# Both halves of the token operand, interleaved by k at fixed places modulo 256 bytes

## What is computed

```python
h = rmsnorm(x, g_pre)                        # x: 288 tokens x 2048
proj = einsum('btd,dn->btn', h, w_in)        # w_in: 2048 x (10 * 2048 + 16)
q, k, v, o, za, ig, fg, u, vb, zb, ga, gb = split(proj)
...                                          # mLSTM on q,k,v (8 heads of 256); spatial gating on u,vb
y_a = sigmoid(o) * hn * silu(za)
y_b = spatial_gating(u, layernorm(vb)) * silu(zb)
merged = sigmoid(ga) * (y_a @ w_pa) + sigmoid(gb) * (y_b @ w_pb)
y = x + rmsnorm(merged @ w_out, g_post)
```

## Time and profile before

| | |
|---|---|
| median of 3 runs | 1470.55 us (1470.46 to 1470.95) |
| the profiled execution's own time | 1470.46 us |
| span of the profile | 1469.0 us |
| TensorE busy with matmuls | 1453.8 us, 99% of the span |
| VectorE, ScalarE, GpSimd busy | 863.1, 622.6, 189.5 us |
| granted TensorE clock, mean | 0.997 |

### The profile page before, as it was taken

The page is one execution under the profiler, slowest core; times in us unless marked ns, Lnnn a source line. Parts: engine busy times, 40 slices in busy tenths (PEclk is TensorE's granted clock), DMA queues, the critical chain, the costliest instruction groups (busy, mean ns, idle before and its releaser), DMA issues. The chain is left out here.

```text
span 1469.0 us, 31016 instructions
## 1 busy us (share of the span) xinstructions
PE 1453.8 (99%) x11115; PEld 1432.7 (98%) x11115; DVE 863.1 (59%) x1418; ACT 622.6 (42%) x869; POOL 189.5 (13%) x340
## 2 busy tenths in 40 slices
PE   9999999999999999999999999999999999999996
PEld 9999999999999999999999999999999999999996
DVE  7756555564444437586767676767676544444444
ACT  6433343343333334454544444445454433333442
POOL 4000000001000000404040414141412000000000
PEclk9999999999999999999999999999999999999998
DMA  7764655557555568696969696969696665655553
GB/s 230 227 155 138 180 161 166 162 151 248 179 174 171 183 184 212 168 293 175 303 166 301 173 305 171 302 174 300 173 289 165 216 174 178 176 177 191 170 156 138
DMA packets 310679, 292.14 MB, mean 199 GB/s; under 512 B 82881, under 2 KB 297609, under 8 KB 309841
## 3 DMA queue, kind: packets, MB, share of 16 engines
q1 hardware_dynamic: 291424, 243.05, 59.1%
q0 software_dynamic: 18960, 48.48, 9.7%
q10 hardware_dynamic: 256, 0.10, 0.0%
HBM read 266.11 MB, written 25.44 MB: 198 GB/s over the span
## 5 line engine op out<-in xcount | busy, mean ns | idle before, releaser
L1066 DVE TENSOR_TENSOR wlo<-raw,whi 128x1024 fp32r<-128x1024 f32 x416 | 506.8, 1222 | 525.3 <-ACT whi L802 523.7
L453 PE MATMUL ps<-xh,whi 128*128 128x288 f32 x2560 | 762.8, 298 | 0.0
L454 PE MATMUL ps<-xl,whi 128*128 128x288 f32 x2560 | 757.4, 296 | 0.0
L455 PE MATMUL ps<-xh,wlo 128*128 128x288 f32 x2560 | 753.8, 294 | 0.0
L802 ACT ACTIVATE whi<-raw 128x1024 fp32r<-128x1024 f32 x416 | 439.3, 1058 | 690.4 <-PE ps L455 656.1
L453 PEld LDWEIGHTS ps<-xh,whi 128*128 128x128 f32 x2560 | 481.4, 188 | 4.9 <-issue 2.9
L454 PEld LDWEIGHTS ps<-xl,whi 128*128 128x128 f32 x2560 | 481.2, 188 | 0.4
L455 PEld LDWEIGHTS ps<-xh,wlo 128*128 128x128 f32 x2560 | 481.1, 188 | 0.0
L453 PE MATMUL ps<-yh,whi 128*128 128x288 f32 x512 | 151.4, 296 | 0.0
L454 PE MATMUL ps<-yl,whi 128*128 128x288 f32 x512 | 151.4, 296 | 0.0
L455 PE MATMUL ps<-yh,wlo 128*128 128x288 f32 x512 | 150.4, 294 | 0.0
(11 more groups left out here) (345 smaller groups left out, 1020.7 us busy)
## 6 DMA issues: line engine op xcount, KB each, us to landing
raw<-in_w_in_dram SPq DMA_DIRECT2D x320, 512.0 KB, 3.9
raw<-in_w_pb_dram SPq DMA_DIRECT2D x32, 512.0 KB, 3.5
Cin<-in_state_mlstm_C_dram POOLq DMA_DIRECT2D x16, 1024.0 KB, 8.4
Xb<-in_state_mlstm_C_dram SPq DMA_DIRECT2D x256, 64.0 KB, 3.8
out_dram<-Cin POOLq DMA_DIRECT2D x16, 1024.0 KB, 6.4
raw<-in_w_pa_dram SPq DMA_DIRECT2D x32, 512.0 KB, 3.5
raw<-in_w_out_dram SPq DMA_DIRECT2D x32, 512.0 KB, 3.6
bcs<-rows_d POOLq DMA_DIRECT2D x8, 304.0 KB, 3.7
```

Of the source, the lines that this page charges most:

```text
L453: nc.tensor.matmul(out, whi[:, c, kk, cols], mh_[:, k, :], start=(k == 0), stop=False)
L454: nc.tensor.matmul(out, whi[:, c, kk, cols], ml_[:, k, :], start=False, stop=False)
L455: last = nc.tensor.matmul(out, wlo[:, c, kk, cols], mh_[:, k, :], start=False, stop=(k == KT - 1))
L1066: nc.vector.tensor_tensor(wlo[:, c], raw[:, c], whi[:, c].bitcast(F32), ALU.subtract).then_inc(lo_ready, 1)
```

## The change

The two halves of each token operand become one tensor with k outside and the half inside: `xx[P, KT, 2, T]`, of which `xh` and `xl` are views, and so `yy` and `mm`. Row k of the upper half now starts at base + 2,304 k and that of the lower half 1,152 bytes after it. 2,304 is 9 times 256, and `moving` now gives an address that is 64 modulo 256, so the upper rows are at phase 64 for every k and the lower rows at phase 192. The weights' area is rounded to 256 instead of 128; it was at 0 modulo 256 before and stays there, one step of 256 further up, and all behind it moves by 256 bytes too. No instruction is added or taken away; addresses and, for writes of two k at once, the distance between the two rows change (2,304 bytes in place of 1,152).

```diff
     def moving(at):
-        return (at + 63) // 128 * 128 + 64
+        return (at + 191) // 256 * 256 + 64
 
     fixed = Area(moving(base))
-    xh = fixed("xh", [P, KT, T], F32R)
-    xl = fixed("xl", [P, KT, T], F32R)
-    fixed = Area((fixed.at + 127) // 128 * 128)
+    xx = fixed("xx", [P, KT, 2, T], F32R)
+    xh, xl = xx[:, :, 0, :], xx[:, :, 1, :]
+    fixed = Area((fixed.at + 255) // 256 * 256)
...
-    yh = y_("yh", [P, KT, T], F32R)
-    yl = y_("yl", [P, KT, T], F32R)
+    yy = y_("yy", [P, KT, 2, T], F32R)
+    yh, yl = yy[:, :, 0, :], yy[:, :, 1, :]
...
-    mh = a("mh", [P, KT, T], F32R)
-    ml = a("ml", [P, KT, T], F32R)
+    mm = a("mm", [P, KT, 2, T], F32R)
+    mh, ml = mm[:, :, 0, :], mm[:, :, 1, :]
```

## The result

The changed kernel takes 1479.05 us, median of 6 runs (1478.67 to 1479.86), against 1470.55 us before: ratio 1.0056, 95% interval 1.0046 to 1.0066. It is slower by 8.5 us: the interval lies above 1.

What follows compares the result with a forecast made beforehand. The prediction took TensorE's matmul pitch as the bound: 1470.5 us less 14.0 us for the moving operand's new phases, all else counted as nothing, gave 1456.5 us. The range was 1432 to 1480 us, the likeliest case's own 1446 to 1467.

Steps and rivals of the forecast that it cites:

- the 0.2% that I had called no change: Whole kernel time: 0.2%, 2.9 us, was about what a measurement can tell from no change.
- The bound: TensorE: nothing keeps it waiting, so the time is the number of matmuls, 9,984, times their pitch, mean 132.5 ns.
- Supply, writes and DMA: Weight supply has over half its time to spare; ScalarE and VectorE writes of two k and DMA transfers: nothing counted.
- gate_sums: Its 32 matmuls would change under 0.1 us; its 131.9 ns pitch was read as one unit saved per phase change pair.
- The unit: Matmul pitch moves in steps of 16 columns, 64 bytes, 16 cycles, 6.67 ns, below 133.33 ns.
- part (1): Moving operand, all 9,984 matmuls: a phase change pair every three matmuls saves one 6.67 ns step, 131.1 ns, -14.0 us.
- (a): Rival on matmul pitch: phase changes save two 6.67 ns steps per pair, 128.9 ns, 1434.5 us; chance 0.18.
- Part (4): Weight loads: weights keep their phase; the new order of moving phases against them was left in the uncertainty, no size.
- Rival (b): Matmul pitch: the phase itself counts, 64 cheap and 192 dear (1469.5 us), or phases do not count (1470.5); chance 0.17.
- Rival (c): Matmul pitch: a change saves only what a run of one phase built up, so 133.33 ns, 1478.8 us; chance 0.20.
- (d): Matmul pitch: a single matmul at 192 between two at 64 costs one step more, 135.6 ns, 1501 us; chance 0.08.

Runs made afterwards that it cites:

- b_h64l192: Layout and order of the kernel before, upper rows read from those at 64, lower rows from those at 192 (wrong rows): 1479.03 us, before 1470.62.

## Why two thirds at the good place save nothing

In the changed kernel two of three matmuls stand at relative 64, and all pay 133.33. Three runs on that:

> Changed kernel; the lower row's matmul comes first of the three (lower with whi, upper with whi, upper with wlo). The sequence of phases is the same but for where it begins (192 64 64); what differs is which weights are loaded beside it. If the sequence of phases alone decides: 133.33 ns, 1479 us. If it matters that the lower row stands between two upper ones with the same weights before it: another pitch, down to 132.2 ns, 1468 us.

> Changed kernel; in one k first the four matmuls with the upper row, then the two with the lower row: runs of four at 64 and two at 192, still two thirds at 64. If what the good phase saves is lost because runs are too short: less than 133.33 ns, 132.2 at best, 1468 us. If runs of even length lose it (runs of two did): 133.33 ns, 1479 us.

> Layout and order of before, upper rows read from those at 192, lower rows from those at 64 (wrong rows, weights at 0). Against the weights this is the sequence that the changed kernel had with its weights at 128. If the relative place and its sequence decide: that kernel's 132.5 to 132.6 ns and 1472 us. If only the share of matmuls at relative 64 counts (a third): 132.9 ns or more, 1475 us.

```diff
-    [(kk, j, w) for kk in range(CK) for j in range(2) for w in (0, 1, 2)]
+    [(kk, j, w) for kk in range(CK) for j in range(2) for w in (1, 0, 2)]
...
+    [(kk, j, w) for kk in range(CK) for j, w in ((0, 0), (0, 2), (1, 0), (1, 2), (0, 1), (1, 1))]
```

(The first new order is a_lfirst, the second a_run4, both in the changed kernel; b_h192l64 is the layout of before with PHASES = (192, 64).) 1478.33, 1477.78 and 1471.67 us, beside 1470.85. In that order:

```profile
380.00:523.00 143.00, 143.00 (x1074) 143.00 (x1074) 57.55 (x50) 51.01 (x51) 2.71 (x5) 1.00 0.57 175
```

```profile
380.00:523.00 143.00, 143.00 (x1074) 143.00 (x1074) 57.42 (x51) 50.89 (x51) 2.71 (x5) 1.00 0.57 175
```

```profile
380.00:523.00 143.00, 143.00 (x1080) 143.00 (x1080) 58.51 (x50) 50.74 (x52) 2.72 (x5) 1.00 0.58 175
```

133.4, 133.4 and 132.7 ns. So it isn't which weights are loaded beside the lower row, nor that the lower row stands alone. That runs of even length lose the saving, the other branch for a_run4, fits runs of two and four but not those of six and twelve. And b_h192l64, with one third at the good place, saves where two thirds don't; it agrees with the changed kernel with moved weights (1472.34 us, the same count of 1,080), which has the same relative sequence 192 64 192. The price of a matmul isn't a sum over places: the sequence has its own.

## Three kernels with all their work

None of these leaves out or changes any product. The first keeps every row at relative place 64 against its own slice, by giving the weight slices of odd k another phase than those of even k:

```diff
...
-    whi = fixed("whi", [P, CHUNKS, CK, PW], F32R)
+    fixed = Area(fixed.at + 128)
+    whi = fixed("whi", [P, 2, 8 * PW + 32], F32R)      # even k, then odd k 128 bytes further on; wlo too
...
-        return (at + 63) // 128 * 128 + 64
+        return (at + 63) // 256 * 256 + 192
```

> Correct kernel. Token operands in the layout of before, but yh and mh moved so that all of them begin at 192 modulo 256; whi and wlo keep the slices of even k from 128 modulo 256 and those of odd k from 0. So every token row starts 64 past the place of its weight slice modulo 256, whatever k. If the relative place sets the pitch: 131.7 ns as in the run with weights at 128 and rows at 192, and the time that it had, 1463 us, a ratio of 0.995. If it only held because all rows and all slices stood still: 132.5 ns or more, 1470 us.

1472.83 us against 1470.85, ratio 1.0011, interval 1.0002 to 1.0020. Its stretch:

```profile
380.00:523.00 143.00, 143.00 (x1079) 143.00 (x1078) 58.48 (x50) 50.52 (x52) 2.71 (x5) 1.00 0.57 175
```

132.8 ns, one unit in twelve. The expected 131.7 didn't come. While the last matmul of a k runs, the slice being loaded is the next k's, 128 bytes off in phase; one load in six is at relative 192. That this breaks the pattern is argued from the schedule and not shown by a run of its own.

The second has the token operands at 0 modulo 128, weights at 0 (the diff of the section on the weights' place), and the order of before, so relative places 128 and 0 alternate by k:

> Correct kernel: layout and order of before with the token operands at 0 modulo 128, so that rows start in turn at 128 and at 0 modulo 256, six matmuls each. If only relative place 192 is dear: 131.7 to 132.2 ns, 1463 to 1468 us, faster than before. If 128 is dear as well: like before, 132.2 to 132.8 ns, 1468 to 1473 us, or 133.33 ns and 1479 us if the changes of place cost what the good phase saves.

1473.56 us against 1470.68, ratio 1.0019, interval 1.0010 to 1.0028. Its stretch:

```profile
380.00:523.00 143.00, 143.00 (x1079) 143.00 (x1078) 58.47 (x50) 50.53 (x52) 2.72 (x5) 1.00 0.56 175
```

132.8 ns. A six at 0 and a six at 128 save one unit between them, no more than 64 and 192 in their slow pattern.

The third is the order with runs of three, timed:

> Correct kernel: layout of before, TensorE's order with runs of three (one k and one j, then k+1), timed. The single look gave 1468.1 us with 132.2 ns a matmul in nearly every chunk. Both theories expect the ratio to the kernel before at 0.998 and to hold in every run, since no disturbance enters it.

1469.28 us against 1471.39, ratio 0.9984, interval 0.9975 to 0.9993. Of the versions executed more than once this is the only one that beats both kernels, by 0.16%, which is just inside the 0.2% that I had called no change. (Runs of one matmul, also with all their work, had 1468.48 us in their single run.) Its gain fits its counts: it stays at two units in twelve also where the kernel before is at one, 1,084 against 1,079 in the MB stretch.

## Why the prediction was wrong

**The bound: right.** The pitch of 9,984 matmuls sets the time. Supply, writes and DMA are as costed, at nothing, and so is `gate_sums` (31 distances in 4.10 us, before 4.09); TensorE's waits are the same; 0.83 ns x 9,984 = 8.3 us is the whole change.

**The unit: right, as far as the counts tell.** All sequences have pitches of 133.33 ns less a number of 6.67 ns units in 12 or 24 matmuls, and no stretch reads higher than 133.4, which is 133.33 within a count.

**The failed step: part (1), "if one such pair saves one unit (6.67 ns, the slow pattern and `gate_sums`), the pitch is 133.33 - 6.67 / 3 = 131.1 ns".** The saving was laid to the change of phase. The term was -14.0 us and measured +8.3: 400.0 ns a triple in place of 393.3, where before it was 397.5. Matmuls that all stand at 64 save two to three units in twelve without any change, and a change after every second matmul saves next to nothing. What drew me there was `gate_sums`: 31 distances with weight slices of 104 columns, 416 bytes from k to k+1, so their place modulo 256 moves with k. It wasn't the same experiment at all; I took it for one, since I held the weights' place to be no part of it. (And the argument against (a) had a count wrong: `gate_sums` changes phase three times as often as the chunks, not six.)

**Part (4), "the weights keep their phase".** True of the layout, and the wrong question. The place of one against the other was left among the uncertainties. It sets the price where all matmuls are alike; where places mix, the sequence does too.

**Rival (b): half right.** The phase has its price, but not additively: by (b) two thirds at 64 would have left the time at 1469.5 us. The rules of the Trainium skill that stood beside it (SBUF — State Buffer, Operand start alignment: multiples of 4 bytes; Door 1: The DMA port swizzle: lines of 16 bytes) can't tell 64 from 192 or 0 from 128; the runs do, by 13 and 17 us of kernel time.

**Rival (c): right number, wrong reason.** 1478.8 forecast, 1479.05 measured, at a chance of 0.20; that the number fits is luck. Runs of one matmul, for which it has 133.33 ns, had 132.2. Its pitch comes about because the sequence 64 192 64 saves no unit, which b_h64l192 shows in another layout; why it saves none is open. (a) and (d) are out.

**What stays open.** Why a sequence saves what it does. Units saved in twelve matmuls, against the weights: all at 0: 3. All at 64: 3 or 2. All at 128 or 192: 0. Of 64 and 192 in turn, runs of 1: 2; of 2: 0; of 3: 2; of 6: 2 or 1; of 12: 1. 0 and 128 in turn, runs of 6: 1. 64 192 64: 0. 192 64 192: 1 to 1.5. Four at 64, two at 192: 0. I have no rule that gives this list. That moving read and weight load get in each other's way in a place modulo 256 bytes fits the pure cases and the exchange of roles; how, isn't shown. And the places explain no more than 1.7 ns: at its best a matmul still takes 131.7 ns, 11.7 more than its 288 columns at 2.4 GHz, and no run here says for what.

Why the same sequence can settle in two patterns is open too, but the trace of the kernel before shows where it turns. The first matmul of each of the first four pairs of MB:

```profile
346.30 0.30 PE L453 MATMUL ps<-xh,whi 128*128 128x288 f32 x1
...
358.99 0.29 PE L453 MATMUL ps<-yh,whi 128*128 128x288 f32 x1
...
371.73 0.29 PE L453 MATMUL ps<-xh,whi 128*128 128x288 f32 x1
...
384.48 0.30 PE L453 MATMUL ps<-yh,whi 128*128 128x288 f32 x1
```

The first x pair takes 12.69 us for its 96 matmuls, 132.2 ns; the y pair behind it 12.74 and the next x pair 12.75, 132.7 and 132.8. An x pair ends at 64 and a y pair begins at 64, so here for the first time twelve matmuls in a row stand at one phase. That this turn is what brings the slow pattern is a guess that no run tests.

## What to carry to other kernels

When one engine is never idle and its instructions are all alike, read the distance between starts over a long stretch and compare it with the length of the operand: what lies between is the only thing that a change of layout can win. Before reading a cause from where that distance varies, let a run hold the suspected quantity still: all at one phase would have told at once what I took from the mixture. And a phase is one of two operands against each other: move the other one too.

## What the hardware showed that I had not expected

The pitch of back-to-back float32r matmuls of 128 weight columns and 288 moving columns, at the granted clock of 1.00, depends on where the moving row starts against the weight slice modulo 256 bytes: 131.7 ns at 0, 131.7 to 132.2 at 64, 133.3 at 128 and at 192, with the number, shape and order of the matmuls the same and TensorE without a wait in the stretch. Mixed places don't average: 64 192 64 costs 133.33 and 192 64 192 costs 132.7, though two of three are at the good place in the first and one in the second. And the same sequence can run in two patterns, 132.2 and 132.8 ns, each kept for hundreds of matmuls.
